# A streaming encoder step: the first expert's rows built by TensorE from the stream, and the router fed from the unscaled stream

## The reference

```
h = h + cross_attn(rmsnorm(h, norm_x), ...)
t = rmsnorm(h, norm_ffn)                       # rsqrt(mean square) per token, times norm_ffn per channel
g_logits = t @ w_router_group + b_router_group           # 4 groups, the best is taken
e_logits = t @ w_router_expert + b_router_expert         # 8 experts in the group, the best two
for e in range(32):
    hid = silu(t @ w_gate[e]) * (t @ w_up[e])            # 1024 -> 256
    out = out + (hid @ w_down[e]) * combine[:, e:e+1]    # 256 -> 1024, zero for tokens not routed to e
h = h + out
```

## Time and profile before

| | us |
|---|---|
| median of 3 runs | 857.23 (856.76 to 858.02) |
| the profiled execution | 854.42 |
| its span, first to last instruction | 852.7 |
| PE busy, share of the span | 792.4, 93% |
| DVE busy | 468.3, 55% |
| mean granted TensorE clock | 0.968 of 2.4 GHz |

### The profile page before, as it was taken

One profiled execution on the slowest core, in us unless ns is written; L12 is line 12 of the kernel. 1 busy time (PEld: TensorE's weight loads), 2 busy tenths in 40 slices (PEclk: granted clock), 3 DMA queues, 4 the chain that ended last, 5 costly groups with the idle time before them and its releaser, 6 DMA issues. The chain is left out here.

```text
span 852.7 us, 21343 instructions
## 1 busy us (share of the span) xinstructions
PE 792.4 (93%) x8993; PEld 648.8 (76%) x8993; DVE 468.3 (55%) x1112; ACT 204.9 (24%) x457; POOL 104.0 (12%) x169
## 2 busy tenths in 40 slices
PE   5999999889999999999999998599999999999926
PEld 3778877867888888777888886587788788888712
DVE  5999986326541142401223445566677777777725
ACT  5002325433221000112222211122222222222213
POOL 1000100203120000000000000122223223223100
PEclk9999999998999999999999999599999999999967
DMA  9531441220213910421021242869999999999645
GB/s 326 211 84 30 63 191 49 67 98 5 95 50 136 402 42 1 164 84 49 1 100 75 98 151 99 339 253 374 382 400 408 395 393 396 397 384 394 255 150 209
DMA packets 43654, 166.30 MB, mean 195 GB/s; under 512 B 16336, under 2 KB 21328, under 8 KB 26768
## 3 DMA queue, kind: packets, MB, share of 16 engines
q1 hardware_dynamic: 32912, 150.36, 46.6%
q0 software_dynamic: 6144, 9.45, 3.4%
q10 hardware_dynamic: 4544, 5.72, 1.9%
HBM read 156.80 MB, written 17.88 MB: 205 GB/s over the span
## 5 line engine op out<-in xcount | busy, mean ns | idle before, releaser
L868 PE MATMUL bank<-act_a,weight_ring 128*128 128x288 f32 x640 | 157.3, 406 | 0.5 <-ACT act_a L1413 0.5
L2277 DVE STREAM_TRANSPOSE region_t<-region_r 32x128 f32<-32x128 f32 x372 | 151.4, 407 | 6.8 <-DMA region_r<-ffn_rows,gather_now 0.6
L868 PEld LDWEIGHTS bank<-act_a,weight_ring 128*128 128x128 f32 x640 | 120.9, 190 | 33.3 <-ACT act_a L1413 0.6
L1156 PE MATMUL bank<-weight_ring,act_b 128*128 128x256 f32 x512 | 111.8, 379 | 0.0
L1156 PEld LDWEIGHTS bank<-weight_ring,act_b 128*128 128x128 f32 x512 | 96.8, 190 | 13.0
L1732 DVE TENSOR_TENSOR region_u<-region_u,bank 128x512 f32<-128x512 f32 (+1 forms) x26 | 17.8, 686 | 90.2 <-PE bank L1156 66.9
L1337 PEld LDWEIGHTS bank<-region_t,weight_ring 128*64 128x64 f32 x1536 | 55.0, 139 | 4.9 <-issue 4.5
L1337 PE MATMUL bank<-region_t,weight_ring 128*64 128x80 f32 x1536 | 57.1, 234 | 1.7 <-issue 1.4
L2246 DVE TENSOR_REDUCE score_max<-bank 128x2 f32<-128x512 f32 (+1 forms) x10 | 6.4, 636 | 65.8 <-PE bank L1196 62.0
L1337 PEld LDWEIGHTS bank<-region_t,region_g 128*64 128x64 f32 x1024 | 36.6, 138 | 5.3 <-issue 5.3
L1337 PE MATMUL bank<-region_t,region_g 128*64 128x80 f32 x1024 | 38.8, 234 | 1.8 <-issue 1.8
(11 more groups left out here) (353 smaller groups left out, 1187.2 us busy)
## 6 DMA issues: line engine op xcount, KB each, us to landing
weight_ring<-in_w_chunks SPq DMA_DIRECT2D x28, 1024.0 KB, 7.8
weight_ring<-in_w_up SPq DMA_DIRECT2D x17, 1024.0 KB, 11.2
weight_ring<-in_w_down SPq DMA_DIRECT2D x10, 1024.0 KB, 9.7
region_g<-in_w_up SPq DMA_DIRECT2D x8, 1024.0 KB, 11.5
region_g<-in_w_gate SPq DMA_DIRECT2D x8, 1024.0 KB, 9.4
conv_io<-in_w_gate SPq DMA_DIRECT2D x8, 1024.0 KB, 11.0
conv_io<-in_w_down SPq DMA_DIRECT2D x8, 1024.0 KB
weight_ring<-in_w_gate SPq DMA_DIRECT2D x7, 1024.0 KB, 9.7
```

Source lines behind the costliest of these rows:

```text
L868: m = pe.matmul(ps[:, 0:HALF], slot(c)[:, k, P * (mt % 2):P * (mt % 2 + 1)], x[:, k, HALF * h:HALF * (h + 1)], start=(k == 0), stop=(k == ...
L1156: m = pe.matmul(ps[0:L, CW * cc:CW * (cc + 1)], x[:, k, t0:t0 + L], slot(c)[:, k, :], start=(k == 0), stop=(k == KD - 1))
L2277: m = dve.transpose(xgT[b][DB * part:DB * (part + 1), 0:4, DB * blk:DB * (blk + 1)], xg[b][DB * blk:DB * (blk + 1), CW * part:CW * (part + 1)]
```

## The change

1. PE turns H itself, unscaled (`turn_stream`), where it turned the scaled rows; it need not wait for `normed`. The router's weights are multiplied once by the gain (`route_gained`), and the reciprocal root is applied by DVE to the logits in `choose`. The turn of tile 3 moves into the middle of the last `token_tile`.
2. Expert 0's rows are not gathered: DVE's `choose_first(t)` makes for each tile a matrix token by slot that holds the reciprocal root where a token has that slot at expert 0, and PE's `first_rows(t)` multiplies H by it, eight matmuls for each tile, over five tiles, into two banks. DVE copies the two banks with the gain into xgT[0]. `turn_first`, `copy_first` and ACT's copy are dropped for expert 0.
3. The order changes. PE: `first_rows` between ranks and slot tables; `total` behind `gate_up(0)`; `down_rows(0)` ahead of `turn_x(1)`. DVE: tile 4's scaling between the `choose_first`s; `dve_hidden(0)`, `expert_gates` and `dve_rows(0)` all ahead of both halves of the turn for expert 1. POOL gathers experts 1 and 2 first.
4. DVE works on both of a token's choices in one instruction in `choose` and `place`. Scratch tiles move from region_t to region_r, whose second half holds the experts' output rows.

```diff
+        last = t == NT - 1
+        if last:
+            for h in range(2):
+                add("fT", "act", t - 1, h)
...
+    for h in range(2):
+        add("first", "dve", h)
...
-                for n in range(3):
-                    gather(n, 0, p, reused=n >= 2)
+                if again:
+                    for n in range(3):
+                        gather(n, 0, p, reused=n >= 2)
+                else:
+                    for n in range(1, 3):
+                        gather(n, 0, p, reused=False)
+                    pool.sem_inc(gx_copied, 1)
...
             def route_earlier(t):
+                if t == NT - 1:
+                    turn_stream(t - 1)
                 if t == 2:
-                    pe.wait_ge(route_loaded, 16)
+                    pe.wait_ge(route_gained, 1)
                 if t >= 2:
                     route_tile(t - 2)
                 if t >= 3:
                     rank_tile(t - 3)
+            def turn_stream(t):
+                L = TOK[t][1]
+                for h in range(2):
+                    ps = claim("fT", t, h)
+                    wait_emptied(pe, "o", t, h)
+                    for k in range(4):
+                        m = turn(ps[:, P * k:P * k + L], H[0:L, t, P * (4 * h + k):P * (4 * h + k + 1)])
+                    m.then_inc(filled, 1)
+
             def o_tile(t):
                 wait_emptied(pe, "pv", NT + t)
                 if t < NT - 1:
                     route_earlier(t)
                 token_tile("o", CH_O, mix, t, between=lambda: route_earlier(t))
-                if t >= 1:
-                    turn_rows("fT", t - 1, NORM_F, TOK[t - 1][1])
...
+            def first_rows(t):
+
+                L = TOK[t][1]
+                pe.wait_ge(first_chosen, t + 1)
+                for k in range(KD):
+                    m = pe.matmul(first_ps[k // 4][:, CAP * (k % 4):CAP * (k % 4 + 1)], H[0:L, t, k::KD],
+                                  first_oh[0:L, t, :], start=(t == 0 and k % 4 == 0),
+                                  stop=(t == NT - 1 and k % 4 == 3))
+                    if t == NT - 1 and k % 4 == 3:
+                        m.then_inc(filled, 1)
+
+            route_tile(NT - 2)
+            turn_stream(NT - 1)
+            first_ps = [claim("first", h) for h in range(2)]
+            first_rows(0)
+            route_tile(NT - 1)
+            rank_tile(NT - 3)
+            first_rows(1)
+            rank_tile(NT - 2)
+            first_rows(2)
             ps = claim("slots")
-            for t in range(NT):
+            for t in range(2):
+                pe.wait_ge(oh_ready, t + 1)
+                slot_table(ps, t)
+            first_rows(3)
+            rank_tile(NT - 1)
+            first_rows(4)
+            for t in range(2, NT):
                 pe.wait_ge(oh_ready, t + 1)
                 m = slot_table(ps, t)
             m.then_inc(filled, 1)
-            ps = claim("total")
-            pe.matmul(ps[:, 0:NE], ones[:, :], before[:, NT - 1, :], start=True, stop=False)
-            for k in range(2):
-                m = pe.matmul(ps[:, 0:NE], ones[0:NS, :], ind[k][0:NS, NT - 1, :], start=False, stop=(k == 1))
-            m.then_inc(filled, 1)
-            for who in ("act", "dve"):
-                pe.wait_ge(emptied[who], count[who])
+
+            def last_use_emptied(*numbers):
+                for j in range(len(plan) - 8, len(plan)):
+                    if j % 8 in numbers:
+                        who, m = rank[j]
+                        pe.wait_ge(emptied[who], m)
...
-                pe.wait_ge(idx_ready, p + 1)
-                turn_first(N0 // 2 if not again else p * (NE // 2), p)
+                if again:
+                    pe.wait_ge(idx_ready, p + 1)
+                    turn_first(p * (NE // 2), p - 1)
+                else:
+                    pe.sem_inc(turned_x, 1)
+                    last_use_emptied(2, 3)
                 gate_up(N0, 0, 0, p, reused=again)
+                if not again:
+                    ps = claim("total")
+                    pe.matmul(ps[:, 0:NE], ones[:, :], before[:, NT - 1, :], start=True, stop=False)
+                    for k in range(2):
+                        m = pe.matmul(ps[:, 0:NE], ones[0:NS, :], ind[0:NS, NT - 1, k, :], start=False, stop=(k == 1))
+                    m.then_inc(filled, 1)
+                    last_use_emptied(4, 5)
+                    down_rows(N0, 0, 0, p, reused=False)
+                    last_use_emptied(0, 1, 6, 7)
                 turn_x(p * (NE // 2), 1)
-                down_rows(N0, 0, 0, p, reused=again)
+                if again:
+                    down_rows(N0, 0, 0, p)
                 gate_up(N0 + 1, 1, 0, p)
...
             turned("fT", NT - 2, xT, *TOK[NT - 2])
+            turned("fT", NT - 1, xT, *TOK[NT - 1])
             o_tile(NT - 1)
-            turned("fT", NT - 1, xT, *TOK[NT - 1])
...
-                copy_x(first, 0)
+                if again:
+                    copy_x(first, 0)
...
                 if first == NORM_F and t == NT - 1:
-                    k = first + t
-                    dve.wait_ge(rstd_ready, k + 1)
-                    link(dve.reciprocal(stat[0:L, k, 16:17], stat[0:L, k, 15:16]))
-                else:
-                    wait_emptied(dve, stage, t, 1)
-                    stats(first + t, H[0:L, t, :], L)
+                    return
+                wait_emptied(dve, stage, t, 1)
+                stats(first + t, H[0:L, t, :], L)
                 if t >= 3:
-                    wait_filled(dve, turned, t - 3, 1)
                     if first == NORM_F:
                         dve.wait_ge(f_stored[t % 3], 16)
+                    else:
+                        wait_filled(dve, turned, t - 3, 1)
                 scale_rows(first + t, rows[0:L, t % 3, :], H[0:L, t, :], g, L)
...
+                dve.wait_ge(cols_loaded, 16)
+                dve.wait_ge(route_loaded, 16)
+                tt(w_rt[:, :, :], w_rt[:, :, :], gain_f.unsqueeze(2).to_broadcast([P, KD, NG + NE]))\
+                    .then_inc(route_gained, 1)
...
-                step(tt(lg_g[0:L, t, :], ps[0:L, 0:NG], b_rt[0:L, 0:NG], ALU.add))
-                tt(lg_e[0:L, t, :], ps[0:L, NG:NG + NE], b_rt[0:L, NG:], ALU.add).then_inc(emptied["dve"], 1)
+                rstd = stat[0:L, NORM_F + t, 16:17]
+                step(dve.scalar_tensor_tensor(lg_g[0:L, t, :], ps[0:L, 0:NG], rstd, b_rt[0:L, 0:NG], ALU.mult, ALU.add))
+                dve.scalar_tensor_tensor(lg_e[0:L, t, :], ps[0:L, NG:NG + NE], rstd, b_rt[0:L, NG:], ALU.mult, ALU.add)\
+                    .then_inc(emptied["dve"], 1)
...
-                for k in range(2):
-                    m = dve.tensor_scalar(ind[k][0:L, t, :], prio[0:L, :], prs[:, k:k + 1], None, ALU.is_equal)
-                m.then_inc(ind_ready, 1)
+                tt(ind[0:L, t], prio[0:L, :].unsqueeze(1).to_broadcast([L, 2, NE]),
+                   prs.unsqueeze(2).to_broadcast([L, 2, NE]), ALU.is_equal).then_inc(ind_ready, 1)
...
+            def choose_first(t):
+
+                L = TOK[t][1]
+                miss, at = r_miss[0:L, 0:1], r_miss[0:L, 1:2]
+                link(dve.tensor_scalar(miss, ind[0:L, t, 0, 0:1], ind[0:L, t, 1, 0:1], -1.0, ALU.add, ALU.add))
+                ps = wait_filled(dve, "rank", t)
+                link(dve.scalar_tensor_tensor(at, miss, SKIP, ps[0:L, 0:1], ALU.mult, ALU.add))
+                dve.tensor_scalar(first_oh[0:L, t, :], slot_id[0:L, :], at, stat[0:L, NORM_F + t, 16:17],
+                                  ALU.is_equal, ALU.mult).then_inc(first_chosen, 1)
+                dve.wait_ge(first_chosen, t + 1)
             def place(t):
                 L = TOK[t][1]
                 ps = wait_filled(dve, "rank", t)
-                for k in range(2):
-                    step(tt(r_sel[0:L, :], ind[k][0:L, t, :], ps[0:L, 0:NE]))
-                    sync()
-                    m = dve.tensor_reduce(r_k[k][0:L, t, :], r_sel[0:L, :], AX.X, ALU.add)
-                    if k == 0:
-                        link(m)
-                m.then_inc(emptied["dve"], 1)
+                link(tt(r_at[0:L], ind[0:L, t], ps[0:L, 0:NE].unsqueeze(1).to_broadcast([L, 2, NE])))
+                dve.tensor_reduce(r_k[0:L, t, :], r_at[0:L], AX.X, ALU.add).then_inc(emptied["dve"], 1)
                 wait_emptied(dve, "rank", t)
-                for k in range(2):
-                    m = dve.tensor_scalar(oh[k][0:L, t, :], slot_id[0:L, :], r_k[k][0:L, t, :], None, ALU.is_equal)
-                    if k == 0:
-                        link(m)
-                m.then_inc(oh_ready, 1)
+                tt(oh[0:L, t], slot_id[0:L, :].unsqueeze(1).to_broadcast([L, 2, CAP]),
+                   r_k[0:L, t, :].unsqueeze(2).to_broadcast([L, 2, CAP]), ALU.is_equal).then_inc(oh_ready, 1)
             def o_tile(t):
                 if t >= 2:
                     choose(t - 2)
                 if t >= 3:
+                    choose_first(t - 3)
                     place(t - 3)
...
```

(58 more changed lines are left out.)

50 lines of the change are left out of this document (24 added, 26 removed).

## The result

The changed kernel took 867.24 us (median of 6 runs, 865.19 to 873.87); the kernel before, run between them, 857.00 (6 runs, 855.13 to 859.91). The ratio is 1.0123, with an interval of 1.0090 to 1.0157: 10 us slower. The forecast was 858.7 with a range to 863.5, so it was wrong, and by more than its range. The profiled executions stand at 867.48 (span 865.7) and 854.42 (span 852.7), 13 us apart; the one of before is 2.6 under its median, the one of after 0.2 over its own, and that is what 13 has over 10.

A forecast was written before the change was run, and what follows sets the result against it. PE was taken as the bound, losing time to waits and half clock at the seam; -5.2 -2.35 +6.7 +2.35 gave +1.5 us, so 858.7. Own range 856.5 to 861.5; with rivals 854.3 to 863.5.

The forecast's parts named there:

- the price of a pass: In first_rows, strided weight loads cost 0.15 us a pass, 2.4 us a tile of 16 passes; 1.7 and 3.0 kept.
- The upper bound: In first_rows, a float32 load pays the stride on top of its own 0.108 (+0.08): 0.19 a pass, 3.0 us a tile.
- the chain: PE's and DVE's steps from first_rows(0) at 531.0 to expert 0's gate and up, starting at 548.2 instead of 553.44.
- The clock: PE hardly stands still from 528.5, so expert 0's gate and up run at 2.4 GHz: 4.65 us, ending at 552.85.
- Rival A: The clock falls already in the routing, slowing PE's new matmuls and expert 0's gate and up: +6.6, 865.3; chance 0.16.
- Rival B: In first_rows the strided load costs nothing, 1.7 us a tile: sum -0.2, 857.0, no change; chance 0.20.
- The standstill ahead of expert 1: Behind turn_x(1), PE waits 5.4 us for DVE's queued turn of expert 1's rows, and its clock falls.
- the end carried to the last expert: Whatever moves the end of expert 1's gate and up, 568.4 us, moves the kernel's end by as much.
- the -5.2: At the seam, expert 0's gate and up start 5.2 us earlier, at 548.2 instead of 553.44.
- the +6.7: Between experts 0 and 1, both halves of the turn queued behind DVE's gates take back 6.7 us.
- the two terms of the clock: Full clock in expert 0's gate and up saves 2.35 us; clock lost in expert 1's gate and up costs 2.35.
- Rival C: Expert 1 keeps 2.4 GHz or regains it within 1 us: -0.9, or -2.6 with loads at 1.7, 854.6; chance 0.22.

The follow-up runs named there:

- f2_best: Not tied to a run in the text; by its number probably contiguous channels, halves, PE's order and DVE's product ahead of the turn on the changed kernel, 0.9942.
- the two last versions: Changed kernel with halves, PE's order, DVE's product first: one with contiguous channels and tile 4's rows stored early, 847.83; the other keeping stride and weight layout, 0.9930.

## Why the prediction was wrong

The step that failed is the price of a pass: "I take 2.4, the row with the same stride, and keep 1.7 and 3.0". It measured 4.0, outside both bounds.

**Where 0.15 came from.** The row was the turn of gathered rows, four passes in 0.60 us. PE's timeline of the kernel before, in windows that start inside these four, shows what a pass in a row costs there:

```profile
560.61 0.50 PE L849 MATMUL bank<-ident,region_r 80*128 80x80 f32 x3
...
560.83 0.27 PE L849 MATMUL bank<-ident,region_r 80*128 80x80 f32 x1
```

The second pass starts 0.17 behind the first (560.43), and the fourth 0.22 behind the second, so the last two are 0.11 apart. So 0.15 was the start of a group, averaged over four passes. Nor is 0.11 the price of a stride: turns of contiguous channels start 0.109 apart with 128 moving columns and 0.062 with 64 (tile 4), which on a straight line is 0.074 for the 80 here (an estimate). By it the stride cost this turn 0.04 a pass, and it cost the matmul's pass 0.13. The upper bound, "if a float32 load pays it on top of its own 0.108 (+0.08)", took its penalty from the same row. No row showed a strided load of a float32 matmul, and no bound allowed that its pass could double.

- *What is open in it.* The turn loads 128 columns at the same stride as `first_rows`, and its passes go at 0.11 where those of `first_rows` go at 0.24. The moving columns are 80 in both, and the smaller number of partitions is not the reason: `first_rows` of the last tile, with 64, goes at 0.24 as well. What differs is the kind of instruction, a transpose in a single pass against a float32 matmul in two. Why that matters was not tried.
- *What that moved.* PE spent 20.3 us in `first_rows` where 12 were counted. Expert 0 started at 559.41 and not at 548.2: 11.2 late, 11.6 from the anchor. From the start of `first_rows(0)` to there it took 28.7 us for 17.2; 7.7 of the difference are the passes (19.7 by the next start, for 12), and 3.8 the router, ranks, tables and one wait of 0.66 between them, nearly all at half clock.
- *A term at nothing.* The slot tables of tiles 2 to 4 stand on PE ahead of expert 0's gate and up, and the chain leaves them out. At full clock they would have hidden beside DVE's copies (an estimate: ten took 1.7 us in `f2_best`, so six take 1.0); at half clock they took 1.98 and ended last, 1.4 behind the copy. With contiguous loads expert 0 started at 547.95 (29.62 from the anchor, forecast 29.63), but partly by luck: the passes and the waits between them took less than counted up to the rank of tile 4 (1.2 from the anchor), and the last tile and the tables, at half clock, gave it back.
- *The clock.* "As PE hardly stood still since 528.5, at 2.4 GHz" failed with it: it fell at 533.59, 2.9 us into the first strided tile, with PE busy all the 2.92 us before. Gate and up of expert 0 took 7.0 and not 4.65: 2.35 more. With contiguous passes in the same order the clock held until 544.08. In the two-half versions with PE's order, gate and up of expert 0 ran at full clock.
- *Rival A* had the event and, by luck, nearly the total (865.3). Its working was wrong: it charged the half clock 1.0 us a tile, and the strided passes cost the same at either clock. The 0.25 was in none of the cases.
- *Rival B*, a free strided load, is refuted. Its 857.0 is about what the contiguous version took, with passes of 0.12 for its 0.108 and part of expert 0 at half clock.
- *What held.* The standstill ahead of expert 1: 5.24 for 5.4; the way from the end of expert 0's gate and up to the start of expert 1: 9.9 for 10.0; gate and up of expert 1 in the fallen clock: 7.0 for 7.0; the end carried to the last expert, within 1.1 us. Of the sum, the -5.2 and the +6.7 are in the contiguous version as forecast (-5.2, +6.6); the two terms of the clock are smaller there, -1.0 for -2.35 and +1.9 for +2.35. It sums to +2.3 where +1.5 was forecast, and its time can't be told from no change.

Sum against the forecast's end of gate and up of expert 1 (569.85, measured 583.3): 11.2 for the start, 2.35 for the clock in expert 0, -0.1 behind. Rival C asked what the start of expert 0 is worth when DVE's queue and the clock don't take it back; the profile allowed a positive answer that the prediction didn't work out with an order of DVE's work: the two last versions win 0.8 and 0.7%.

What stays open: why the clock falls under a full queue of strided passes, why a strided pass takes 0.11 us in the turn and 0.24 in the matmul, what the standstills put down to "issue" inside gate and up are, and why the clock fell upstream in some executions and not in others, which moves them by up to 7 us.

## What to carry to other kernels

Before a float32 matmul takes its stationary operand at a stride, count the words that it uses of 16 bytes: at strides of 4 and 8 float32 words a pass took 0.24 us where it took 0.12 at 1 and 2, and at half clock it took no less. Read it in another order, or cut it into two column halves. Take the price of a pass from the distance between starts inside a long group, not from the length of a short one, and from an instruction of the same kind. When work is moved out of a stall, ask at once what stood in that stall's shadow (here DVE's turn, and the gather behind full queues): three versions gained the start of expert 0 and gave it back there. Compare profiles from an anchor ahead of the changed place, not by their spans.

## What the runs showed of the hardware

- A float32 matmul pass of 128 stationary and 80 moving columns, in a stream of such passes: 0.121 us at strides of 1 and 2 words, 0.24 at 4, 0.25 at 8, the last two the same at a granted clock of 1.00 and 0.50. The Trainium skill, "TensorE: Matmul & The Clock Gate", section "LDWEIGHTS (loading the stationary operand)", prices a load by its columns alone, 107 ns for 128. The contiguous pass, 0.112 from start to start, is near it; at 4 words and more the measurement decides against it.
- A contiguous pass of this kind goes by the clock: 0.11 us at 1.00, 0.21 at 0.50.
- Transposes by PE (one pass each) of 128 columns at full clock started 0.111 us apart with 80 partitions and a stride of 8 words; with contiguous columns 0.109 with 128 partitions and 0.062 with 64.
- Two loads of 64 strided columns into different halves of the array overlap: 2.0 us a tile for 4.0, and 1.2 for 2.0 with contiguous channels at full clock.
- The clock fell while PE was busy without a gap: 2.92 of 2.92 us in the kernel after, 2.15 of 2.16 with the stride of 4. With two halves of the same strided data it kept 1.00 until 546.38, 13.5 us after the first pass, in the change's order; in PE's other order it had fallen at 533.56, 0.27 us ahead of the first pass, behind waits of 0.38, 0.29 and 0.56 us.
- A store of 256 KB among weight loads (queues at 1.0 of their time) took 6.4 to 8.2 us from issue to landing over the twelve profiles. One of the first two gathers, of 80 rows, took 5.3 to 7.8 where the weight loads ran on, and 2.4 to 4.2 where they had ended or ended within 2 us of its issue; issuing the first 2.4 us earlier under full queues brought the rows no earlier.
